# Decode attention inside a decoder step on one core: new values' product in quarters, maxima before scores, page copies earlier, and another order of the first sample

## The reference, cut to what matters

```
def fox_attention(q, k, v, logf, q_offset):
    c_k = jnp.cumsum(logf.astype(jnp.float32), axis=1).transpose(0, 2, 1)
    ...
        s = jnp.einsum('bqhd,bkhd->bhqk', q_blk, k).astype(jnp.float32) * scale
        c_q = jnp.take(c_k, q_pos, axis=2)
        s = s + c_q[..., :, None] - c_k[..., None, :]
        s = jnp.where(key_pos[None, :] <= q_pos[:, None], s, -jnp.inf)
        p = jax.nn.softmax(s, axis=-1).astype(v.dtype)
        return jnp.einsum('bhqk,bkhd->bqhd', p, v)
```

## Time and profile before

| | us |
|---|---|
| three runs, median (lowest to highest) | 2663.24 (2662.0 to 2663.32) |
| the profiled execution's own time | 2660.18 |
| its span in the trace | 2658.5 |
| TensorE busy with products | 2572.5, 97% |
| VectorE, ScalarE, GpSimd busy | 1241.5, 873.6, 410.6 |

### The profile page before, as it was taken

The page is one execution under the profiler, slowest core; times in us unless marked ns, Lnnn a source line. Parts: engine busy times, 40 slices in busy tenths (PEclk is TensorE's granted clock), DMA queues, the critical chain, the costliest instruction groups (busy, mean ns, idle before and its releaser), DMA issues.

```text
span 2658.5 us, 51458 instructions
## 1 busy us (share of the span) xinstructions
PE 2572.5 (97%) x20485; PEld 2438.9 (92%) x20485; DVE 1241.5 (47%) x2018; ACT 873.6 (33%) x1542; POOL 410.6 (15%) x602
## 2 busy tenths in 40 slices
PE   8999999998998999999999999999989989999998
PEld 7999999995556999999999999989979969999998
DVE  5444325545554544442444442378646565444423
ACT  4222224214443422232332232244354444222322
POOL 0000003023332200000200000065335542000001
PEclk9999999998999999999999999999999999999999
DMA  4232322247885233233222233223210133332331
GB/s 127 88 88 87 101 81 67 78 130 257 288 294 186 63 91 90 87 100 88 59 87 88 87 103 89 67 64 87 74 36 1 33 98 95 94 88 87 100 88 45
DMA packets 397765, 263.17 MB, mean 99 GB/s; under 512 B 10984, under 2 KB 370613, under 8 KB 397608
## 3 DMA queue, kind: packets, MB, share of 16 engines
q1 hardware_dynamic: 386096, 223.03, 28.9%
q0 software_dynamic: 11536, 38.28, 4.3%
HBM read 251.71 MB, written 9.56 MB: 98 GB/s over the span
## 4 chain that ended last, share of the span: by engine, by line
PE 69%; DVE 4%; ACT 2%; issue 1%; POOL 1%; ACTq 0%; POOLq 0%; DVEq 0%
PE ps L495 50%; PE ps L481 4%; PE ps L2388 2%; PE ps L1445 1%; PE ps L2404 1%; PE ps L1499 1%; PE ps L1458 1%; PE ps L1469 1%; POOL xT L1026 1%; PE ps L538 1%; PE ps L2412 1%; PE ps L509 1%; PE ps L1392 0%; PE ps L2372 0%; PE ps L1414 0%
## 5 line engine op out<-in xcount | busy, mean ns | idle before, releaser
L473 DVE TENSOR_TENSOR w_lo<-w_raw,w_hi 128x1024 fp32r<-128x1024 f32 (+1 forms) x314 | 422.4, 1345 | 970.5 <-ACT w_hi L466 968.8
L495 PE MATMUL ps<-hd_hi,w_hi 128*128 128x272 f32 x3712 | 771.1, 289 | 4.4 <-DVE w_lo L473 4.3
L495 PE MATMUL ps<-hd_lo,w_hi 128*128 128x272 f32 x3712 | 767.4, 288 | 0.0
L495 PE MATMUL ps<-hd_hi,w_lo 128*128 128x272 f32 x3712 | 763.5, 287 | 0.0
L466 ACT CAST w_hi<-w_raw 128x1024 fp32r<-128x1024 f32 (+1 forms) x314 | 351.0, 1118 | 1122.6 <-PE ps L495 1068.0
L495 PEld LDWEIGHTS ps<-hd_hi,w_hi 128*128 128x128 f32 x3712 | 581.1, 188 | 7.8 <-issue 7.4
L495 PEld LDWEIGHTS ps<-hd_lo,w_hi 128*128 128x128 f32 x3712 | 584.4, 189 | 0.0
L495 PEld LDWEIGHTS ps<-hd_hi,w_lo 128*128 128x128 f32 x3712 | 581.8, 188 | 0.0
L1026 POOL TENSOR_TENSOR xT<-xT,rstd_rows 128x272 f32<-128x272 f32 x96 | 84.5, 910 | 1709.7 <-DVE rstd_rows L1051 1709.6
L495 PE MATMUL ps<-h_hi,w_hi 128*128 128x272 f32 x1232 | 255.2, 289 | 0.0
L495 PE MATMUL ps<-h_lo,w_hi 128*128 128x272 f32 x1232 | 254.7, 288 | 0.0
(11 more groups left out here) (529 smaller groups left out, 2985.1 us busy)
## 6 DMA issues: line engine op xcount, KB each, us to landing
w_raw<-in_ffn_w_gate_dram SPq DMA_DIRECT2D x88, 512.0 KB, 3.7
w_raw<-in_ffn_w_up_dram SPq DMA_DIRECT2D x88, 512.0 KB, 3.7
w_raw<-in_ffn_w_down_dram SPq DMA_DIRECT2D x64, 704.0 KB, 4.6
v_pages<-in_cache_a_v_dram POOLq DMA_DIRECT2D x128, 256.0 KB, 4.4
w_raw<-in_c_w_in_dram SPq DMA_DIRECT2D x33, 512.0 KB, 4.0
k_pages<-in_cache_a_k_dram SPq DMA_DIRECT2D x64, 256.0 KB, 4.3
k_pages_raw<-in_cache_a_k_dram SPq DMA_DIRECT2D x64, 256.0 KB, 3.9
w_raw<-in_ab_w_in_dram SPq DMA_DIRECT2D x25, 512.0 KB, 3.9
```

The costliest lines, as they stand in the source:

```text
L473: e.tensor_tensor(w_lo[:, n % 2, 0:nk * P], raw[:, n % RAW, 0:nk * P], w_hi[:, n % 2, 0:nk * P].bitcast(F32), ALU.subtract).then_inc(sem(" ...
L495: mm = e.matmul(ps[:, bank + h, 0:TH], w, x[:, k0 + k, half(h)], start=first and k == 0 and w is wh and x is x_hi, stop=last and k == nk - ...
```

## The change

What it does, by function: `group_scores` no longer waits for s_rows. The product of `new_values` moves into `value_pages`, ahead of its last four pages, as four products of 128 columns, each on its own strip of the array; fold adds the strips as before. In the pass of a sample, TensorE turns the maxima ahead of scores(2b) and page 11 ahead of scores(2b + 1), and spreads the maxima between pages 2 and 3; VectorE does maxima_diag, queries and shift ahead of row maxima, and pages 7, 11 and 13 ahead of a normalising, a row maximum and the output rows. In the first sample, pages 4 to 7 are turned between the turns of probabilities, the tail of the convolution is transposed later, the conv_high casts come behind the turned blocks, and conv_low is spread over VectorE's list. At the end all four prompt_low stand behind shift.

```
-                since(e, "s_rows_ready", b * 4 + G)
                 since(e, "probs_turned", probs_before(b, G))
...
+                    if g == PAGES - 4:
+                        for x in range(4):
+                            at = slice(x * P, (x + 1) * P)
+                            e.matmul(ps[x * NS:(x + 1) * NS, 5, at], p_new, v_rows_s[:, at], start=False, stop=False)
                     e.matmul(ps[j * NS:(j + 1) * NS, 5, :], p_dec[:, g, :], v_page[:, g, :], start=g < 4,
-                             stop=j > 0 and g >= PAGES - 4).then_inc(sem("v_page_used"), 1)
+                             stop=g >= PAGES - 4).then_inc(sem("v_page_used"), 1)
             def new_values(b, last=False):
-                e.matmul(ps[0:NS, 5, :], p_new, v_rows_s[:, :], start=False, stop=True)
...
                 pv(2 * b - 1)
+                maxima_turned(b - 1)
                 scores(2 * b)
                 page_turn(b, 2)
-                maxima_turned(b - 1)
+                maxima_spread(b - 1)
                 page_turn(b, 3)
-                maxima_spread(b - 1)
...
                 pv(2 * b)
+                page_turn(b, 11)
                 scores(2 * b + 1)
-                page_turn(b, 11)
...
+            page_out(0, 5)
+            page_out(0, 7)
+            conv_low(0)
             o_out(0)
             row_maxima(2)
             row_maxima(3)
+            conv_low(1)
+            conv_low(2)
+            new_out(0)
+            group_out(0, 0)
             normalise(2)
             normalise(3)
+            conv_low(3).then_inc(sem("vector_stage"), reached("conv_b_done"))
...
+                maxima_diag(b - 1)
+                queries(b)
                 row_maxima(4 * b)
-                queries(b)
-                maxima_diag(b - 1)
+                shift(b - 1)
                 row_maxima(4 * b + 1)
-                shift(b - 1)
                 normalise(4 * b)
...
                 group_out(b, 1)
+                page_out(b, 13)
                 output_rows(b - 1)
-                page_out(b, 13)
...
-            for i in range(2):
-                prompt_low(i)
             maxima_diag(DEC_B - 1)
             shift(DEC_B - 1)
-            for i in range(2, NP):
+            for i in range(NP):
                 prompt_low(i)
```

More of the change, by code:

```diff
@@ L1525, in pe_ab @@
             group_scores(0, 0)
+            page_turn(0, 4)
             turn(0, 1)
+            page_turn(0, 5)
+            page_turn(0, 6)
+            turn(1, 1)
+            page_turn(0, 7)
+            pv(0)
+            scores(1)
+            group_scores(0, 1)
+            e.wait_ge(sem("o_taken"), 1)
+            new_scores(0)
+            group_turn(0, 0)
             e.wait_ge(sem("conv_b_ext"), MB)
@@ L1530, in pe_ab @@
             mm.then_inc(sem("tensor_stage"), reached("b_tail_psum"))
-            turn(1, 1)
-            pv(0)
-            scores(1)
-            for g in range(4, 8):
-                page_turn(0, g)
-            group_scores(0, 1)
-            e.wait_ge(sem("o_taken"), 1)
-            new_scores(0)
-            group_turn(0, 0)
             turn(2, 2)
```

27 lines of the change are left out of this document (10 added, 17 removed).

## The result

The changed kernel takes 2647.25 us in the median of five executions (2645.13 to 2650.99); the kernel before took 2662.19 us in five beside it (2660.55 to 2663.32). The ratio is 0.9945 with a 95% interval of 0.9933 to 0.9957: faster by 0.55%, near the 2646 forecast. The profiled execution took 2647.25 us with a span of 2645.6, 12.9 less than the span before.

What follows compares the result with a forecast made beforehand. It took TensorE as the bound of decode attention, its standing being all that moving work could win. Loop 9.4, first sample 5 and stage's end 2.5 sum to 16.9 us, from the median 2663.24 to 2646; range 2639 to 2655.

Steps and rivals of the forecast that it cites:

- the terms 9.4 + 5 + 2.5: Forecast gains in us: the loop of seven samples 9.4, the first sample 5, the end of the stage 2.5.
- The product: New values' product as four quarters on four strips: 0.39 instead of 1.04 us, 0.65 us saved, eight times.
- The rival in which they don't overlap: The four quarter products, all reading the same 32 partitions, don't overlap: minus 5.2 us, 2651; chance 0.1.
- Maxima ahead of the scores: In the loop, the wait ahead of L1489 goes; 0.27 us odd, 0.22 even reach the second group, stall moves to L1405.
- the walk: In b = 3, ScalarE's chain of page 3, exp(4b) and page 4: page 4's copy at 692.4 instead of 692.67.
- Page 11 ahead of the scores: In the loop, the wait ahead of the third group's scores goes whole: 0.73 us odd, 0.47 even.
- Pages 5, 7 and 13: Earlier on VectorE: 5 and 7 win nothing; 13 loses 0.3 us in b = 1, 3, 5, 0.2 in b = 7, 0.05 even.
- the walk of VectorE's chain: Turn of page 13 to fourth group's scores: 3.45 to 3.6 us with wide blocks, 3.35 in even samples, against 3.29.
- The first sample: New order starts turn(2) 7.8 us sooner, a shorter low clock costs 2.7: gain 5 us, bounds 4 and 7.8.
- The rival "the clock stays up": Clock stays up in the first sample and the tail: 2.8 + 0.8 us more gain, 2642.5; chance 0.2.
- The end of the stage: prompt_low later and last product shorter give 1.75 us, with half the low clock's cost 2.5; bounds 1.1 and 3.3.
- the sum: Over the kernel: 16.9 us gained, from the profiled 2660.18 us and its 3.06 us under the median, giving 2646.

Runs made afterwards that it cites:

- experiment 8: The changed kernel with the maxima's order of before on TensorE and VectorE; the loop is 0.62 us longer.
- experiment 6: The changed kernel with the four quarter products behind the last value pages; six of seven samples within 0.03 us of the change's, first sample 26.56 us.
- experiment 1: The kernel before with only the new values' product in quarters; ratio 0.9973 (0.9963 to 0.9983), loop 3.53 us shorter.
- experiment 2: The kernel before with only the first sample's new order on TensorE, ScalarE and VectorE; ratio 0.9979 (0.9969 to 0.9989).
- experiment 5: The changed kernel with page 13's copy behind the output rows again; the loop is 0.64 us longer.
- experiment 7: The changed kernel with the last sample's value pages 8 to 15 loaded by SyncE instead of GpSimd; ratio to the kernel before 0.9949 (0.9935 to 0.9963).
- experiment 9: The changed kernel once more, unaltered; 2648.7 us, ratio 0.9953 (0.9939 to 0.9966).
- experiment 10: The changed kernel with the last sample's value pages 8 to 15 loaded by SyncE, measured again; 2646.13 us, ratio 0.9936 (0.9923 to 0.995).
- experiment 4: The kernel before with eleven unread identity products in TensorE's 2.92 us pause of the first sample; 2660.88 against 2661.92 us, ratio 0.9996.

## Why the prediction was right, and where it was not

The time, 2646 forecast and 2647.25 measured, holds. Of the terms 9.4 + 5 + 2.5 the trace shows 7.1 + 8.3 + 0.3. With the 0.6 us by which the stage begins sooner (596.54 and 595.96) that is 16.3 at the stage's end, against 16.9 forecast. That the sum is so near is in part luck: one term 3.3 too small, two 2.3 and 2.2 too large, and a begin of the stage that lies between 594.5 and 596.5 us over the traces, whatever the kernel. Of the 2.3 us that the loop lacks, 1.1 are the maxima's (0.7 for 1.7 forecast), 0.8 page 11's (3.5 for 4.3) and 0.2 the product's (4.35 for 4.55); the loss at page 13 is 1.3 as booked (1.25).

**The product: right.** 0.65 was forecast; it is 0.63 in b = 3. The four quarter products take 0.42 us from start to end, where I had put 0.39 against the 1.04 of the one; from start to start it is 0.35 against 0.97, the same 0.62 less. The rival in which they don't overlap is refuted. The Trainium skill, "TensorEngine Tiling (Array Packing)", section "Theoretical Speedup", gives up to four times for a small side of 32; by that the estimate would be 0.26, a quarter of 1.04, and the trace's factor is 2.5 (2.8 from start to start).

**Maxima ahead of the scores: mechanism right, size off.** The wait ahead of the spread is gone and the stall moved to L1405, as said. The way from the start of pv (L1414) to L1405 is 7.28 us against 7.42 in b = 3, 0.14 won and not 0.27; in b = 2 it is 0.07 and not 0.22. The start-to-start times that the walk lists add up to 691.22 and not 691.27; with the 0.54 and 0.65 of the copy and the exp it still comes to page 4's copy at 692.4. Undoing it costs 0.09 a sample (experiment 8).

**Page 11 ahead of the scores: right, a little large.** From L1405 to the third group's scores 10.68 us against 11.33, 0.65 for 0.73 forecast; 0.3 for 0.47 in the even samples. There page 11's turn starts 0.51 us behind the pv ahead of it (663.04 to 663.55 in b = 2), where the scores started 0.37 behind it; what holds it isn't in the rows.

A piece that both steps lack is what it costs TensorE to change the form of its products. Page 11's turn stood ahead of another page's and now stands ahead of the scores: it holds TensorE for 0.59 us (691.57 to 692.16), where from page to page it is 0.49. The transpose L1484 holds TensorE 0.21 us between pv and scores (677.33 to 677.54), where it stood between pages with 0.11 (679.25 to 679.36 in experiment 8). So 0.1 us each, and there are two more such places in a sample than before. (L1484 counts as a page's like here, whatever the form printed for it: the page ahead of it takes 0.49.) The Trainium skill's same page, section "Key Properties", says that changing the mode drains the engine. The trace fits that, with about 0.1 us at these places. I had used the rule on the product alone, where it costs nothing to speak of (experiment 6). That these 0.1 us are the whole of what is missing in the odd samples is an argument from the rows, not shown by a run; in the even ones they are not the whole (see page 11).

**Pages 5, 7 and 13: wrong.** The prediction said that "the output rows (0.75 us) and the normalising now stand between page 13's copy and page 15's", and booked this as "a **loss of 0.3**". The size is near (0.25 in b = 3, 0.25 in b = 7, 0.11 in the even samples), and so is the walk of VectorE's chain (3.54 us for 3.45 to 3.6); the cause is not: with page 13 back behind the output rows, b = 1, 3 and 5 are 0.25 us longer, not shorter. Only in b = 7 does the move itself cost, 0.11. The lengthening comes from TensorE's being early at a chain of VectorE that had just kept up with it; the product alone brings on 0.14 of it, with VectorE's old order (experiment 1).

**The first sample: size off.** The step that failed is "So 1.8 us may be enough, and I take it that the clock falls once more, for about half as long." The walk itself was good: a standing of 1.8 us forecast, 1.75 measured, turn(2) at 609.3 forecast and at 608.61 measured, of which 0.58 is the earlier begin. The clock stayed at 1.00, and the gain was 8.3 us, not 5, and above the term's upper bound of 7.8: the way behind turn(2) is 0.4 us shorter as well, whose beginning had still run at the lower clock before. The rival "the clock stays up" had named 2.8 us for that, in this stretch. But it was no certain thing: of the eight profiled executions with this standing (the change, experiments 2, 5, 6, 7, 8, 9 and 10) the clock fell in two, at a price of 2.6 and 1.2 us. The forecast had charged 2.7 with certainty; the mean of the eight is 0.5. By the medians of experiment 2 the first sample's order gives 5.8 us, near the 5 forecast. What makes the difference to the trace's 8.3 isn't shown; the profiled executions, one of each kernel, can't tell how often the clock fell in the others.

**The end of the stage: wrong.** "1.1 + 0.65 for the last product = 1.75" overlooks who comes next. The 1.08 us ahead of the spread did go, but TensorE then waits 1.97 us for the value pages 12 to 15, and the stretch at the lower clock behind it is longer. Nothing in my list of what could be late named GpSimd in the last sample; I had worked out its loads for the first sample alone. Experiment 7 shows it, and 10 again: without that wait the end gains 3.4 us, a little over the 3.3 of the upper bound.

**Behind the stage** the sum supposed that nothing changes. Its base was a profiled execution in which the rest took 1804.6 us, the shortest of all; in the change's it took 3.4 more, with a lower granted clock in stretches that the diff doesn't touch. The forecast started at 2660.18 less 16.9, and came back to the median with the 3.06 us between them. By the medians 14.9 us were won and by the stage's marks 16.3. Of the 1.4 between them 0.6 are the earlier begin of the stage; whether the rest is chance or has a cause, no run here tells.

## What to carry to other kernels

A stall in the list of waits is worth only what the next chain leaves of it: walk on to the instruction that all engines need next, and count to there (4.6 us of stall in the loop were worth 0.6). When one engine gets faster everywhere, look at the last pass of a loop for the engine that loads its data by itself: its chain doesn't shrink, and there is no later pass to hide it. Splitting a product with few rows over the array's strips pays as the rows show (from start to start 0.97 to 0.35 us). Where the clock has fallen behind a pause, closing most of the pause won 3.8 us in one trace, nearly as much as the new order, but only 1.0 in the medians: measure several executions before you count on it.

## What the runs showed of the hardware

- The same work behind the stage took 1804.6 to 1811.0 us in thirteen traces.
- Behind the same pause of 1.74 or 1.75 us TensorE's clock stayed at 1.00 in six executions and fell in two, at once in experiment 10 and 1.5 us later in 6; with one and the same kernel it did both (experiments 7 and 10). Behind 2.92 or 2.93 us it fell in all three traces, at a price of 2.4 to 4.0 us against experiment 4; with 0.86 us or with products in the pause it did not.
- Eight records for four products of 128 columns on four strips with 32 rows each, all reading the same 32 partitions, take 0.42 us, and the next product starts 0.35 us behind the first; one product of 512 columns takes 1.04, and the next starts 0.97 behind it.
- A transpose ahead of a product of another form holds TensorE about 0.1 us longer than ahead of another transpose (0.59 against 0.49, 0.21 against 0.11).
- GpSimd issues value-page loads one in 1.14 us in the first sample, one in 1.31 in the loop and one in 1.16 in the last sample, there with 3.13 us of pause behind the first; SyncE issued eight in 8.40 us, one in 1.05.
- An instruction of VectorE on 384 columns took 0.50 us in one execution and 1.95 in another, in which two of GpSimd's ran in the same time (experiment 6).
